# Top-256 selection by bit-wise counting passes in place of eight-at-a-time extraction

## The reference

```
score = jnp.einsum('bth,bths->bts', iwb, sc).astype(jnp.float32)
admissible = key_chunk[None, :] <= (tpos // CHUNK)[:, None]
score = jnp.where(admissible[None], score, -jnp.inf)
vals, sel = lax.top_k(score, topk)          # topk = 256
```

## Time and profile before

| | |
|---|---|
| median of 3 runs | 2620.8 us (2618.99 to 2628.22) |
| profiled execution | 2619.45 us, its span 2617.6 us |
| busy in the span | PE 93%, DVE 67%, POOL 56%, ACT 45% |
| mean granted clock of PE | 0.978 |
| PE's share of the chain that ended last | 66% |

### The profile page before, as it was taken

The page is one execution under the profiler, slowest core; times in us unless marked ns, Lnnn a source line. Parts: engine busy times, 40 slices in busy tenths (PEclk is TensorE's granted clock), DMA queues, the critical chain, the costliest instruction groups (busy, mean ns, idle before and its releaser), DMA issues.

```text
span 2617.6 us, 34947 instructions
## 1 busy us (share of the span) xinstructions
PE 2432.2 (93%) x11680; PEld 1999.3 (76%) x11680; DVE 1761.4 (67%) x2933; ACT 1189.7 (45%) x2025; POOL 1471.8 (56%) x821
## 2 busy tenths in 40 slices
PE   7899999798898999999999999977989999999997
PEld 6689877577676788888788887866777888878886
DVE  5599999867566477656565687156649565566676
ACT  5443533456556165444443326255546444434331
POOL 2111787544643317887678741446634888587951
PEclk9999999799999999999999999999999999999999
DMA  5480733633343653454754434655463545654343
GB/s 148 65 121 25 153 95 111 209 101 101 110 133 103 221 171 101 145 164 133 243 187 161 145 112 146 149 153 125 109 205 97 149 139 170 207 208 150 119 137 129
DMA packets 323427, 369.62 MB, mean 141 GB/s; under 512 B 13827, under 2 KB 221731, under 8 KB 320981
## 3 DMA queue, kind: packets, MB, share of 16 engines
q1 hardware_dynamic: 313796, 350.38, 45.7%
q10 hardware_dynamic: 9216, 16.78, 2.2%
q0 software_dynamic: 272, 0.62, 0.1%
HBM read 237.18 MB, written 130.55 MB: 140 GB/s over the span
## 4 chain that ended last, share of the span: by engine, by line
PE 66%; issue 14%; DVE 9%; POOL 5%; ACT 4%; DMA 2%; DVEq 1%; SPq 0%; POOLq 0%; ACTq 0%
PE ps L442 63%; POOL attn_out_split L1164 2%; POOL attn_out L1162 2%; PE ps L2528 1%; DVE masks L1994 1%; DVE max L1990 1%; DVE probs_T L2104 1%; DVE logits L2069 1%; DVE masks L1973 1%; POOL attn_out_split L1160 1%; DMA h_operand_raw<-h_operand_scratch 1%; ACT relu_scores L1426 1%; ACT probs_T L1577 1%; POOL attn_out_low L1157 1%; DVE acc L1806 1%
## 5 line engine op out<-in xcount | busy, mean ns | idle before, releaser
L442 PE MATMUL ps<-xn_T,w_split 128*128 128x512 f32 (+1 forms) x2928 | 679.2, 391 | 6.1 <-ACT x_sums L1309 5.5
L442 PEld LDWEIGHTS ps<-xn_T,w_split 128*128 128x128 f32 (+1 forms) x2928 | 548.0, 188 | 124.7 <-issue 4.6
L442 PE MATMUL ps<-w_operand,h_operand 128*128 128x512 f32 x2016 | 464.5, 393 | 10.4 <-DVE acc L2325 6.8
L398 POOL TENSOR_TENSOR w_split<-w_raw,w_split 128x1024 fp32r<-128x1024 f32 x80 | 195.4, 2453 | 479.0 <-ACT w_split L391 478.7
L442 PEld LDWEIGHTS ps<-w_operand,h_operand 128*128 128x128 f32 x2016 | 382.2, 190 | 92.7 <-issue 10.4
L1186 POOL TENSOR_TENSOR w_split<-w_raw,w_split 128x512 fp32r<-128x512 f32 x168 | 241.8, 1450 | 104.9 <-ACT w_split L1669 103.4
L442 PE MATMUL ps<-x_sums_high,w_split 128*128 128x512 f32 x896 | 285.0, 389 | 0.0
L2327 DVE TENSOR_TENSOR acc<-acc,ps 128x512 f32<-128x512 f32 x288 | 185.9, 681 | 129.6 <-PE ps L442 129.1
L1218 POOL TENSOR_TENSOR w_operand<-w_block,w_operand 128x2048 fp32r<-128x2048 f32 x42 | 207.8, 4947 | 111.4 <-ACT w_operand L1689 111.4
L442 PE MATMUL ps<-w_split,hidden 128*128 128x512 f32 x960 | 224.0, 394 | 9.3 <-POOL w_split L398 6.3
L442 PEld LDWEIGHTS ps<-w_split,hidden 128*128 128x128 f32 x960 | 182.0, 190 | 48.6 <-issue 6.7
(11 more groups left out here) (262 smaller groups left out, 4233.0 us busy)
## 6 DMA issues: line engine op xcount, KB each, us to landing
h_operand_raw<-h_operand_scratch SPq DMA_DIRECT2D x42, 1024.0 KB, 5.3
w_raw<-in_w SPq DMA_DIRECT2D x72, 512.0 KB, 8.1
w_block<-in_w SPq DMA_DIRECT2D x48, 512.0 KB, 5.7
q_scratch<-q_split SPq DMA_DIRECT2D x128, 128.0 KB, 2.5
q_tile<-q_scratch ACTq DMA_DIRECT2D x64, 256.0 KB, 2.7
cat_scratch<-attn_out_split SPq DMA_DIRECT2D x128, 128.0 KB, 2.7
w_raw<-in_w_in SPq DMA_DIRECT2D x30, 512.0 KB, 5.0
h_operand_scratch<-h_even SPq DMA_DIRECT2D x14, 1024.0 KB, 4.4
```

The source lines that it names most:

```text
L398: nc.gpsimd.tensor_tensor(whl[:, n0 % 4, 1, :], wraw[:, n0 % 4, :], whl[:, n0 % 4, 0, :].bitcast(F32), ALU.subtract).then_inc(w_lo, 1)
L442: return nc.tensor.matmul(out_ap, stat, mov, start=start, stop=stop)
```

## The change

The selection no longer takes out values. It finds, for each query, the bit pattern of the 256th largest score, beginning with the sign bit. `bound` holds a candidate per query and row (an int32, read as float32). In each of 32 rounds all six rows are counted: a TENSOR_SCALAR compares the row with its bound (is_ge), writes one byte per key to `flag` (two buffers in turn), and adds the flags to `above[:, k]`. Two operations on 128 x 6 then compute from the six counts whether the bit stays (`turn`) and form the next bound. After the round of bit 18, the 14th, comes the gate's normaliser. After 32 rounds `select(k)` treats each row: count the greater ones, mark the equal ones, number those by a scan that begins at the count, keep the equal ones up to number 256, add the greater ones, and turn the result into 0 or 1e30. `flag` lies where `bias_lines` is, so the DVE first waits for the two stores (`line_sp`). The loops are unrolled, with no hardware loop.

```diff
+    flag = at("sel_flag", [P, 2, 1024], U8, D0 + 86 * K)
     lines = at("bias_lines", [48, REL_SPAN], F32, D0 + 86 * K)
...
-            with dve.Fori(0, TOPK // 8 // 4, 1) as i:
-                for r in range(4):
-                    c = base + 4 * r + 16 * i
-                    for e in range(2):
-                        dve.wait_ge(tk, c + e + 1)
-                        own_wait(dve)
-                        nc.vector.max(m8[:, e], rows[e]).then_inc(tk, 1)
-                    for e in range(2):
-                        dve.wait_ge(tk, c + e + 3)
-                        own_wait(dve)
-                        nc.vector.match_replace(rows[e], m8[:, e], rows[e], NEG_SEL).then_inc(tk, 1)
-            tkc[0] += TOPK // 2
-            for e in range(2):
-                dve.wait_ge(tk, 2 + tkc[0])
-                nc.vector.tensor_scalar(rows[e], rows[e], -2.0e38, MASKED, ALU.is_ge, ALU.mult).then_inc(mask_ok, 1)
-
-        dve.sem_inc(tk, 2)
-        topk((7, 2))
-        dve.wait_ge(ln_sq, 1)
-        rstd(rsv, sdv, sqv)
-        nc.vector.tensor_tensor(nmr[:], negmu[:], rsv[:], ALU.mult).then_inc(ln_nm, 1)
-        topk((6, 3))
-        topk((5, 4))
+        picks = (7, 6, 5, 4, 3, 2)
...
+        def count(k, op, bounds):
+
+            n = issued[0]
+            dve.wait_ge(tk, max(bounds, n - 1))
+            return tick(nc.vector.tensor_scalar(flag[:, n % 2, 0:(picks[k] + 1) * P], row(picks[k]), bound[:, k:k + 1].bitcast(F32), None,
+                                                op, ALU.add, accum_out=above[:, k:k + 1]))
...
+            greater, equal = flag[:, 0, 0:w], flag[:, 1, 0:w]
+            dve.wait_ge(tk, issued[0])
+            tick(nc.vector.tensor_scalar(greater, row(b), bound[:, k:k + 1].bitcast(F32), None, ALU.is_gt, ALU.add, accum_out=above[:, k:k + 1]))
+            n = tick(nc.vector.tensor_scalar(equal, row(b), bound[:, k:k + 1].bitcast(F32), None, ALU.is_equal))
+            dve.wait_ge(tk, n)
+            n = tick(nc.vector.tensor_tensor_scan(row(b), equal, equal, above[:, k:k + 1], ALU.add, ALU.bypass))
+            dve.wait_ge(tk, n)
+            n = tick(nc.vector.scalar_tensor_tensor(row(b), row(b), float(TOPK), equal, ALU.is_le, ALU.mult))
+            dve.wait_ge(tk, n)
+            n = tick(nc.vector.tensor_tensor(row(b), row(b), greater, ALU.add))
+            dve.wait_ge(tk, n)
+            nc.vector.tensor_scalar(row(b), row(b), 0.5, MASKED, ALU.is_lt, ALU.mult).then_inc(mask_ok, 1)
+
+        dve.wait_ge(line_sp, 32)
+        dve.wait_ge(v_ch, chain[0])
+        bounds = tick(nc.vector.memset(bound[:], 0))
+        for bit in range(31, -1, -1):
+            for k in range(len(picks)):
+                counted = count(k, ALU.is_ge, bounds)
+            dve.wait_ge(tk, counted)
+            turned = tick(nc.vector.tensor_scalar(turn[:], above[:], float(TOPK), -1.0 if bit == 31 else float(1 << bit),
+                                                  ALU.is_lt, ALU.mult))
+            dve.wait_ge(tk, turned)
+            if bit:
+                bounds = tick(nc.vector.scalar_tensor_tensor(bound[:], bound[:], 1 << (bit - 1), turn[:], ALU.bitwise_xor, ALU.bitwise_xor))
+            else:
+                bounds = tick(nc.vector.tensor_tensor(bound[:], bound[:], turn[:], ALU.bitwise_xor))
+            if bit == 18:
+                normalizer()
+        for k in range(len(picks)):
+            select(k)
```

More of the change, by code:

```diff
@@ L20 @@
 F32R = mybir.dt.float32r
+U8 = mybir.dt.uint8
+I32 = mybir.dt.int32
 ALU = mybir.AluOpType
@@ L166, in program @@
     nw2 = const("newton2", [P, NB])
-    m8 = const("max8", [P, 2, 8])
+    bound = const("sel_bound", [P, 6], I32)
+    turn = const("sel_turn", [P, 6], I32)
+    above = const("sel_count", [P, 6])
     mx = const("row_min_far", [P, 2, 4])
@@ L2000, in dve_program, with tick, row @@
-        dve.sem_inc(tk, 2)
-        topk((7, 2))
-        dve.wait_ge(ln_sq, 1)
-        rstd(rsv, sdv, sqv)
-        nc.vector.tensor_tensor(nmr[:], negmu[:], rsv[:], ALU.mult).then_inc(ln_nm, 1)
-        topk((6, 3))
-        topk((5, 4))
+        picks = (7, 6, 5, 4, 3, 2)
+        issued = [0]
+        def tick(ins):
+            ins.then_inc(tk, 1)
+            issued[0] += 1
+            return issued[0]
+        def row(b):
+            return masks[:, mask_off(b):mask_off(b) + (b + 1) * P]
@@ new lines, in count, with normalizer @@
+        def count(k, op, bounds):
[3 more added lines that the diff above has]
+                                                op, ALU.add, accum_out=above[:, k:k + 1]))
+        def normalizer():
+            dve.wait_ge(ln_sq, 1)
+            rstd(rsv, sdv, sqv)
+            nc.vector.tensor_tensor(nmr[:], negmu[:], rsv[:], ALU.mult).then_inc(ln_nm, 1)
@@ new lines, in select @@
+        def select(k):
+            b = picks[k]
+            w = (b + 1) * P
+            greater, equal = flag[:, 0, 0:w], flag[:, 1, 0:w]
[10 more added lines that the diff above has]
+            nc.vector.tensor_scalar(row(b), row(b), 0.5, MASKED, ALU.is_lt, ALU.mult).then_inc(mask_ok, 1)
```

## The result

The changed kernel takes 2632.5 us (median of 6 runs, 2632.04 to 2635.54) against 2621.47 us for the kernel before (6 runs, 2618.74 to 2628.22): ratio 1.0044, 95% interval 1.0031 to 1.0057. The forecast was 2632. The profiled execution took 2632.8 us, span 2631.0, mean granted clock 0.973 (before 0.978).

The account below looks back on a forecast made before the run. It took what ends last before the attention, the gate stage or the selection, as the bound: 14 us lost in the gate stage less 3.0 us gained, 11 us added to the 2620.8 us median, gives 2632 us, range 2618 to 2650.

Parts of the forecast that it names:

- What bounds the kernel, ceiling 3.0 us: Before the attention, what ends last counts; all that a faster selection can give is 3.0 us, 0.1% of the time.
- Start: First count waits for the store of bias_lines: 174.3 us in place of 154.1, a new stall of 20 us.
- A round: Six counts, a last read-out and two tiny updates on the DVE take 6.0 us a round.
- Rivals 2 and 3: In the rounds, counts exclude POOL too (7%, 2659 us), or counts run at half rate (5%, 2765 us).
- Updates: Two small DVE instructions per round exclude POOL; waiting adds about 1.7 us a round in the last 18 rounds.
- The small updates ... add 2: From 347 to 407 us, eight rounds' updates delay POOL by 0.2 to 0.3 us each, 2 us together.
- Selects: After the rounds, 30 us of DVE work, 24 excluding POOL, in 30 instructions waiting about 1.2 us each, ending near 475.
- What it does to POOL: In the gate stage, some 15 chain instructions are held 12 us, updates add 2; the stage ends 14 us later.
- Clock: TensorE loses clock after long stalls; one or two stalls above 3 us would add 3 to 7 us.

Follow-up runs that it names:

- e1: Changed kernel with each select cut to one rewriting per row against the bound, ties at the 256th value not broken: 2624.1 us.
- e2: Changed kernel with each select replaced by five unused accumulating counts and one rewriting per row, ties not broken: 2623.3 us.
- e4: Changed kernel with the first 14 rounds' flags in their own place, the wait for the bias-line stores moved behind the normaliser: 2633.7 us.
- e3: Changed kernel with the selects made to wait until POOL has made the last gate output: 2650.3 us.
- e7: Changed kernel with the first three selects each waiting for POOL's v_ln_split of groups 5, 6 and 7, where POOL's chain pauses: 2632.2 us.
- e5: Changed kernel with every instruction of the selects but the first count cut into two of half the columns: 2629.6 us.
- e6: Changed kernel with the scan of each select made twice, one behind the other, same result: 2634.8 us.

## Why the prediction was right

The total was right to 0.5 us, and by the mechanism it names, but several terms of the sum were off, and in opposite directions. (The 0.5%, or 13 us, that it took as the least a measurement can tell was too coarse: the interval is 0.13% either way, and 0.44% is clear of no change.)

- *What bounds the kernel, ceiling 3.0 us.* Right: a selection that ends 22 us earlier (461.0 for 483.4) gives nothing by itself. That the kernel without a hold (e1, e2) gets not even the 3.0 us comes from the gate stage, which ends at 467.4 to 467.8 there instead of 465.3, for the slow U block ahead of the selects. Over the kernels with little or no hold it ends between 465.3 and 470.4, as the granted clock falls in one U block or in three. The selects' share is 9 to 10 us, by which the changed kernel takes longer than e1 and e2, each against its own before.
- *Start.* 174.3 forecast, 175.0 measured, hidden (e4).
- *A round.* 6.0 forecast, 5.73 measured. The 1024-column count is 1.28 us and the read-out is 0.08, nearly all of it hidden. Rivals 2 and 3 fall with it: the counts at L1998 read 601 ns at 384 columns to 1281 at 1024, with POOL at any load.
- *Updates.* Right on the DVE. Minimum, median and maximum in ns of the two lines:

```profile
L2030 DVE TENSOR_SCALAR sel_turn<-sel_count x32: 171/174/2408, 180.4 to 396.0; 128x6 int32<-128x6 f32 x32
L2034 DVE SCALAR_TENSOR_TENSOR sel_bound<-sel_bound,sel_turn x31: 166/167/2318, 180.6 to 390.4; 128x6 int32<-128x6 int32 x31
```

  Six columns wide, they wait up to a whole POOL instruction. The late rounds take 7.4 us (7.7 forecast) and start at 266.3 (269 forecast), so the selects start at 400.35 (407 forecast). The other way round the term was wrong: **"The small updates ... add 2"** to POOL's delay. POOL's rows of 1024 columns up to 400 read 2.34 to 2.42, and e1 keeps all updates and loses about 2 us at most. An instruction of 0.17 us holds POOL for too short a time to matter.
- *Selects.* 30 us of work forecast, 33 measured (e3, less its waits of 3), of which 28 exclude POOL (24 forecast): scan 10.3, the two two-input instructions 11.1, is_equal 3.7 and the rewriting 2.8 over the six rows. The scan streams at half rate: 2.35 us at 1024 columns, 1.02 at 384. They end at 461 and not at 475, as they start 7 us earlier and wait 0.9 us per instruction instead of 1.2 (61 us less 33, over 30 instructions).
- *What it does to POOL*: the term that was mis-sized. **"some 15, each with about one 0.8 us DVE instruction ahead of it: 12 us"** measured 12 instructions at 0.63 us, 7.5 us: 3.1, 2.5 and 1.9 in three iterations. The selects were over before the fourth (461.0, its gate_u starts at 461.63), and the prediction counted each at its full length, though POOL waits only for what is left of it when POOL is ready.
- *Clock.* The prediction left it out of the sum and gave it 3 to 7 us in the bounds. In the stretches of the gate products and U blocks it measured 5.7 us: 3.1 in the product behind the 3.67 us stall (6.8 us instead of 3.73), 1.7 in the next, 0.9 in the last iteration (the slower U blocks between lie beside POOL's chain). Before lost 2.1 us itself in the same stage. The sum of the gate stage, each as the difference to before: 0.6 (already there at 398) + 7.5 + 5.7 - 2.1 = 11.7; measured 11.5. Forecast 14, with the clock at nothing. The right total of 14 less 3.0 is thus partly luck: too much hold and no clock.
- *The remainder.* At the attention the profiled executions are 9.1 us apart, the medians of all runs 11.0, the ends of the two profiled executions 13.4. The last 2 to 4 us come behind the selection. I could not tie them to the change: from the first attention instruction to the end the changed kernel's execution takes 4.3 us more than that of before, and the seven variants' take from 2.4 less (e2, its fastest execution) to 5.4 more (e7), so single executions differ there by as much. Left open.
- *Cause.* Shown: it is the selects' instructions (e1 without them, e2 with the same load in another form), not the start (e4), and not a DVE that ends too late. That POOL is held less by narrower ones (e5) and more by a longer one (e6) is shown by POOL's rows; the times point the same way, with intervals that overlap that of after. Only argued: how much of the 5.7 us of clock the hold causes. Right behind the 3.67 us stall the clock is at 0.50, behind a wait of 2.30 (e5) it falls 2.5 us later, but e3 loses clock in three U blocks with no hold at all. From 402 us on the stage takes 62.8 to 65.2 us in the three kernels without much hold and 64.1 in before, so of the 11.0 us more in after 3.5 stand beside the 7.5 of hold. That the stalls cause them is likely, but it rests on one execution of each.

The Trainium skill ("SBUF — State Buffer", Who interferes with whom) names which DVE forms take the shared port pair and which don't, and the runs agree on each form used here: the accumulating tensor_scalar is free (e2), the two-input instructions and is_equal, a tensor_scalar without accumulator, are not (3.25 and 1.76 us in after against 1.23 and 0.75 in e7). The scan has two inputs, too, and goes with them (4.37 against 2.35).

## What to carry to other kernels

Before making a busy engine faster, look at what ends last behind it: here 3.0 us was all there was to gain, although 328 us of instructions were replaced. Sort the new DVE instructions by form: the accumulating tensor_scalar runs beside a full POOL for free, while two-input instructions, scans and two-column tensor_scalar cost a critical POOL chain up to their own length each, so keep those out of the stage in which POOL is critical, or keep them narrow. Moving them behind that stage is no way out when the DVE then comes last (e3, e7): ask for both ends at once.

## What the runs showed of the hardware

- A DVE and a POOL instruction that exclude each other alternate one by one: beside a full POOL the 1024-column scan reads 4.37 us instead of 2.35, a two-input instruction 3.25 instead of 1.23, is_equal 1.76 instead of 0.75, and the 6-column update up to 2.41 instead of 0.17.
- TensorE's granted clock fell to 0.76 over 6 us in e3 where it was 6.00 of 6 us busy and its last wait had been 0.45 us. Every run had slow U blocks (12.1 to 13.6 us instead of 11.14), before too (12.48 at 432.36, behind a wait of 0.62 us). What brings these falls stays open; they move the end of the gate stage by some 2 to 5 us from one profiled execution to another, as much as several of the effects studied here.
